# A hybrid attention block on one core: the order in which VectorE normalises the recurrence's output and TensorE turns it ahead of the first output projection

## The reference

```python
def mixer_ab(...):
    z = u @ w_in
    ...
    ya = diff_attention(qa, ka, va, lam, subln_g, lambda_init)   # 1024 columns
    yb = rwkv7_time_mix(zb, ...)                                 # 1024 columns
    return jnp.concatenate([ya, yb], axis=-1) @ w_out            # 2048 x 2048

# the end of rwkv7_time_mix: y is the recurrence's output, 16 heads of 64
    mu_y = jnp.mean(y, axis=-1, keepdims=True)
    var_y = jnp.mean(jnp.square(y - mu_y), axis=-1, keepdims=True)
    y = (y - mu_y) * lax.rsqrt(var_y + LNX_EPS)
    y = y * lnx_g + lnx_b
    y = (y + bonus) * g
```

## Time and profile before

| what | value |
|---|---|
| median of 3 runs | 2513.8 us (2513.76 to 2515.22) |
| the profiled execution's own time | 2517.1 us |
| its span in the trace | 2515.4 us |
| PE busy | 2477.1 us, 98% |
| DVE busy | 1502.9 us, 60% |
| ACT busy | 1202.0 us, 48% |
| POOL busy | 150.8 us, 6% |
| mean granted clock of PE | 0.996 of 2.4 GHz |
| stretch of the change | about 440 to 492 us from the span's start |

### The profile page before, as it was taken

The page is one execution under the profiler, slowest core; times in us unless marked ns, Lnnn a source line. Parts: engine busy times, 40 slices in busy tenths (PEclk is TensorE's granted clock), DMA queues, the critical chain, the costliest instruction groups (busy, mean ns, idle before and its releaser), DMA issues.

```text
span 2515.4 us, 32703 instructions
## 1 busy us (share of the span) xinstructions
PE 2477.1 (98%) x13517; PEld 2059.6 (82%) x13517; DVE 1502.9 (60%) x1986; ACT 1202.0 (48%) x1661; POOL 150.8 (6%) x173
## 2 busy tenths in 40 slices
PE   9999999999999999999999999999999999999998
PEld 7888778888888888888888977788888888888886
DVE  5556775766555555555566778556555555555565
ACT  6445432565345345354445556555435445445453
POOL 4001224100000000000100000000000000000000
PEclk9999999999999999999999999999999999999999
DMA  8556511655555555555554654455555565565554
GB/s 275 184 183 209 176 31 70 239 167 186 192 191 186 191 192 184 193 192 193 184 201 147 202 165 151 149 174 184 184 196 189 184 197 189 184 197 188 193 189 146
DMA packets 225145, 454.33 MB, mean 181 GB/s; under 512 B 7897, under 2 KB 16407, under 8 KB 223723
## 3 DMA queue, kind: packets, MB, share of 16 engines
q1 hardware_dynamic: 219165, 430.63, 52.3%
q0 software_dynamic: 3936, 18.59, 2.2%
q10 hardware_dynamic: 1902, 3.07, 0.4%
HBM read 446.57 MB, written 2.10 MB: 178 GB/s over the span
## 4 chain that ended last, share of the span: by engine, by line
PE 92%; DVE 5%; ACT 1%; issue 1%; DMA 0%; SPq 0%; DVEq 0%; ACTq 0%
PE psum L324 28%; PE psum L326 28%; PE psum L325 28%; DVE wlo L303 1%; PE psum L859 1%; PE psum L1882 1%; PE psum L1891 1%; PE psum L483 1%; ACT whi L292 0%; DVE h L678 0%; PE psum L1871 0%; DMA h<-in_x 0%; PE psum L1202 0%; PE psum L1203 0%; PE psum L1204 0%
## 5 line engine op out<-in xcount | busy, mean ns | idle before, releaser
L324 PE MATMUL psum<-whi,uTh 128*128 128x512 f32 (+2 forms) x2176 | 849.9, 391 | 6.3 <-DVE uTl L495 2.1
L326 PE MATMUL psum<-whi,uTl 128*128 128x512 f32 (+2 forms) x2176 | 841.8, 387 | 0.0
L325 PE MATMUL psum<-wlo,uTh 128*128 128x512 f32 (+2 forms) x2176 | 841.0, 386 | 0.0
L303 DVE TENSOR_TENSOR wlo<-raw,whi 128x2048 fp32r<-128x2048 f32 (+1 forms) x243 | 563.9, 2331 | 400.9 <-ACT whi L292 400.9
L292 ACT ACTIVATE whi<-raw 128x2048 fp32r<-128x2048 f32 (+1 forms) x243 | 462.9, 1913 | 414.2 <-DMA raw<-in_w_mlp_down 322.9
L307 DVE SCALAR_TENSOR_TENSOR wlo<-raw,gpre,whi 128x512 fp32r<-128x512 f32 (+1 forms) x656 | 441.7, 735 | 280.0 <-ACT whi L295 279.8
L295 ACT ACTIVATE whi<-raw,gpre 128x512 fp32r<-128x512 f32 (+1 forms) x656 | 414.3, 707 | 269.2 <-DMA raw<-in_w_mlp_up 245.4
L324 PEld LDWEIGHTS psum<-whi,uTh 128*128 128x128 f32 x2176 | 409.0, 188 | 92.9 <-issue 7.2
L326 PEld LDWEIGHTS psum<-whi,uTl 128*128 128x128 f32 x2176 | 408.8, 188 | 81.5
L325 PEld LDWEIGHTS psum<-wlo,uTh 128*128 128x128 f32 x2176 | 409.1, 188 | 78.4 <-issue 0.5
L324 PE MATMUL psum<-whi,hTh 128*128 128x512 f32 x1024 | 399.9, 390 | 0.0
(11 more groups left out here) (379 smaller groups left out, 1504.2 us busy)
## 6 DMA issues: line engine op xcount, KB each, us to landing
raw<-in_w_mlp_up SPq DMA_DIRECT2D x128, 1024.0 KB, 5.5
raw<-in_w_mlp_down SPq DMA_DIRECT2D x128, 1024.0 KB, 5.0
raw<-in_ab_w_in SPq DMA_DIRECT2D x48, 1024.0 KB, 5.2
raw<-in_w_ple_gate SPq DMA_DIRECT2D x32, 1024.0 KB, 5.1
raw<-in_c_w_in SPq DMA_DIRECT2D x24, 1024.0 KB, 5.3
raw<-in_ab_w_out SPq DMA_DIRECT2D x16, 1024.0 KB, 5.3
raw<-in_c_w_out SPq DMA_DIRECT2D x16, 1024.0 KB, 5.1
raw<-in_c_w_in SPq DMA_DIRECT2D x12, 736.0 KB, 4.6
```

Of the source, the lines that this page charges most:

```text
L303: dve.tensor_tensor(wlo[:, q, :, 0:n], raw[:, q, :, 0:n], whi[:, q, :, 0:n].bitcast(F32), ALU.subtract).then_inc(lo_ready, 1)
L324: pe.matmul(o, xh, hi, start=(q == 0 and k == 0), stop=False)
L325: pe.matmul(o, xh, lo, start=False, stop=False)
L326: last = pe.matmul(o, xl, hi, start=False, stop=(q == 3 and k == 3))
```

## The change

Four things are reordered; no instruction is added or removed, and every size stays.

1. DVE, before PE's first matmul of the stage: the rest of the second half of block 0 (`T_dve` 0, part 1) comes ahead of tile 0's Newton steps (k = 3) and no longer behind them.
2. DVE's norm goes by column and no longer by tile: the first column half (k = 4) of both tiles, and only after block 2's turn the second half (k = 5) of both.
3. PE's chunks of v = 1 go (0, 2), (1, 2), (0, 3), (1, 3), so block 3 is first needed by the third of them; block 3 is turned in the middle of v = 1's second chunk and no longer at the end of v = 0's fourth. Block 2 is turned where it was. `y_ready` counts `yb_done` by the new order, and `out_keep_act` of column block 0 waits for one chunk more.
4. ACT: `split_hi` of chunks 2 and 3 comes ahead of the squares of tile 1; `split_hi` of slab s+1's chunks 1 and 2 ahead of block 3's turn; `split_hi` of slab s+2's chunk 0 ahead of the eviction of column block 0.

```diff
-    OUT_CHUNKS = (((0, 0), (0, 1), (1, 0), (1, 1)), ((0, 2), (0, 3), (1, 2), (1, 3)))
+    OUT_CHUNKS = (((0, 0), (0, 1), (1, 0), (1, 1)), ((0, 2), (1, 2), (0, 3), (1, 3)))
@@ out_act
             T_act(act, st, 1)
-            y_square_act(act, 1)
             split_hi(act, s, 2)
             split_hi(act, s, 3)
+            y_square_act(act, 1)
             split_hi(act, s + 1, 0)
             T_act(act, st, 2)
-            T_act(act, st, 3)
             split_hi(act, s + 1, 1)
             split_hi(act, s + 1, 2)
+            T_act(act, st, 3)
             split_hi(act, s + 1, 3)
-            out_keep_act(act, st, 0, 4 * s + 6)
             split_hi(act, s + 2, 0)
+            out_keep_act(act, st, 0, 4 * s + 7)
             split_hi(act, s + 2, 1)
             out_keep_act(act, st, 1, 4 * s + 8)
@@ out_dve
-            out_norm_dve(dve, link, 0, 4)
             T_dve(dve, st, 1)
             out_norm_dve(dve, link, 1, 0)
             out_norm_dve(dve, link, 1, 1)
-            out_norm_dve(dve, link, 0, 5)
+            out_norm_dve(dve, link, 0, 4)
             split_lo(dve, s, 2)
             split_lo(dve, s, 3)
             out_norm_dve(dve, link, 1, 2)
             out_norm_dve(dve, link, 1, 3)
             out_norm_dve(dve, link, 1, 4)
+            split_lo(dve, s + 1, 0)
+            T_dve(dve, st, 2)
+            split_lo(dve, s + 1, 1)
+            out_norm_dve(dve, link, 0, 5)
             out_norm_dve(dve, link, 1, 5)
-            T_dve(dve, st, 2)
-            split_lo(dve, s + 1, 0)
+            split_lo(dve, s + 1, 2)
             T_dve(dve, st, 3)
-            for q in range(1, 4):
-                split_lo(dve, s + 1, q)
+            split_lo(dve, s + 1, 3)
             split_lo(dve, s + 2, 0)
             split_lo(dve, s + 2, 1)
@@ out_pair_pe
-                    if v == 0 and q == 3 and k % 2:
-
-                        if k == 3:
-                            last.then_inc(mm_used, 1)
-                        T_pe(pe, st, src, ready, 2 + k // 2)
-                if v or q < 3:
-                    last.then_inc(mm_used, 1)
+                    if k == 1 and (v, q) in ((0, 3), (1, 1)):
+                        T_pe(pe, st, src, ready, 2 + v)
+                last.then_inc(mm_used, 1)
@@ rwkv_dve
         out_norm_dve(dve, link, 0, 2)
+        T_dve(dve, "ab_out", 0, None, (1,))
         out_norm_dve(dve, link, 0, 3)
-        T_dve(dve, "ab_out", 0, None, (1,))
@@ y_ready
-            return lambda tt, b: (sem("ya_done"), tt + 1) if b < 2 else (sem("yb_done"), 2 * tt + b - 1)
+            return lambda tt, b: (sem("ya_done"), tt + 1) if b < 2 else (sem("yb_done"), 2 * (b - 2) + tt + 1)
```

## The result

The changed kernel takes 2516.97 us (median of 22 runs, 2515.13 to 2524.07), the kernel before 2513.73 us (22 runs, 2512.08 to 2517.04). The ratio is 1.0015, with a 95% interval of 1.0009 to 1.0021: slower, by 2 to 5 us, where 2.4 us less were forecast, and outside the range.

The account below looks back on a forecast made before the run. PE was taken to bound the kernel (92% of the span); PE waits removed, 1.19 + 0.35 + 0.84 = 2.38 us, brought the median from 2513.8 to a forecast 2511.4 us, range 2509.7 to 2514.3.

Parts of the forecast that it names:

- first term: Stage start: block 0's second half made earlier on DVE lets PE begin at 443.69 instead of 444.88, saving 1.19 us.
- The three terms: PE waits removed: 1.19 us at the stage's start, 0.35 us at chunk 3, 0.84 us around block 3's turn.
- The reading that DVE would find ACT's half ready: Block 0's second half: ACT has it at 441.46, before DVE ends the sums of squares at 441.53.
- The load: Slab s+2's chunk 1, issued at 478.6 into POOL's loads, takes 10.8 us, lands at 489.4 and costs nothing.
- its other end: Latest landing of slab s+2's chunk 1: 15.1 us after POOL began, at 493.0, a stall of 2.5 us.
- chunk 1 of slab s+2 lands late: Rival, chance 0.10: PE idles before slab s+2's second chunk; landing at 493.0 gives 2513.9 us, no gain or slower.
- within 0.2%: Whole kernel: chance 0.92 that the time is the same within 0.2% (5.0 us); faster 0.05, slower 0.03.
- The estimate from the page: POOL's loads and slab s+2's chunk: 2.0 us plus 4.46 MB over 436 GB/s from 477.9 ends at 490.1, just in time.
- First matmul 0.8 us behind the turn: Sign at the stage's start: PE's first matmul comes about 0.8 us behind the start of block 1's turn.
- No wait before chunk 3: Sign in the stage: chunk 3's rest is there at 453.1, wanted at 454.75, so the 0.23 us wait goes.
- Turns followed by matmuls at once: Sign: block 2's turn at about 462.9 and block 3's at 474.7 are each followed by matmuls at once.
- one sign of being wrong: Stated failure sign: the prediction is wrong if PE waits in slab s+2; no size given.

Follow-up runs that it names:

- before_gpost_held: Kernel before, with POOL's third load (gpost, 1024 KB) held until slab s+2's chunk 0 is used: 2514.72 us, ratio 1.0000.
- half_turn_alone: Kernel before with only the second half of block 0 moved ahead of tile 0's Newton steps on DVE: 2516.56 us, ratio 1.0006.
- before_pool_ahead: Kernel before with POOL's three loads held to start just ahead of slab s+2's chunk 0: 2516.41 us, ratio 1.0005.
- pool_on_norm: Changed kernel with POOL's three loads let go earlier, by the norm's last half instead of block 3's rest: 2512.59 us, ratio 0.9990.
- gpost_held: Changed kernel with POOL's third load (gpost, 1024 KB) held until slab s+2's chunk 0 is used: 2513.45 us, ratio 0.9990.
- pool_behind: Changed kernel with POOL's three loads held to start behind slab s+2's chunk 1 and ahead of chunk 2: 2514.42 us, ratio 0.9999.
- busy_wait: Changed kernel with 20 useless 128x128 matmuls on PE ahead of the wait for slab s+2's chunk 1: 2516.64 us, ratio 1.0006.
- changed_again: The changed kernel measured once more, without a further edit, beside the kernel before on another chip: 2516.59 us, ratio 1.0008.
- before_pool_late: Kernel before with POOL's three loads held until ACT's high part of slab s+1's last chunk: 2515.04 us, ratio 0.9997.
- norm_and_held_2: Second run: changed kernel with POOL's wple and pin loads let go by the norm's last half, gpost held until s+2's chunk 0 is used: 2512.11 us, ratio 0.9992.

## Why the prediction was wrong

**The stage itself: right in its mechanism, with a first term that one execution had made large.** The three terms, 1.19 + 0.35 + 0.84 = 2.38 us, measured 2.42 us in the changed kernel and 2.45 us where nothing comes after them, each against the one profile of the kernel before. The order of events came within 0.2 us once both are counted from block 1's turn: block 2's turn at 20.03 us (forecast 20.02), block 3's at 31.83 us (31.83), slab s+2 at 46.32 us (46.36). DVE was 0.9 us ahead at both turned blocks (0.8 forecast). But the close agreement is in part luck. The 1.19 us were read in an execution with a low clock in the recurrence; at the full clock the first matmul comes 1.19 us behind the turn even without part 1, so the term is 0.34 us, and the stage's gain 1.61 us (before_gpost_held). The reading that DVE would find ACT's half ready (441.46 against 441.53) had 0.07 us to spare, and the changed kernel's DVE waited 0.84 us for it. That the first term is one sum with the others, and worth nothing alone, was not said, and half_turn_alone shows it.

**The load: the step that failed.** The prediction put it: "With 10.8 us it lands at 489.4 and costs nothing: this value I take, since it is a like load in the same traffic." It was no like load. 10.8 us was the flight of a chunk issued when POOL's loads were 4.3 us under way. The chunk now came 0.8 us behind their first issue and had 3.5 us more of them ahead of it. What stays the same is not the flight but the landing behind POOL's first issue, 15.1 us, the number that the prediction had worked out as its other end and left. With it the landing is 477.9 + 15.1 = 493.0, forecast by its own clock, and 492.1 by the trace's, 0.8 us of which is the earlier recurrence. before_pool_ahead, pool_on_norm, gpost_held and pool_behind each move one side of this and PE's wait follows.

**The price of the wait: too low.** The rival "chunk 1 of slab s+2 lands late" named place and idle time (2.5 us, measured 2.37) but priced it at the idle alone, so that its end was "no change" (2513.9). The wait is also followed by 3 us at half the clock, which cost 1.66 us by the comparison with busy_wait. In the stretch the case costs 4.3 us instead of 2.5, and so lies above the kernel before by 1.9 us. This rival had a chance of 0.10 and should have been the main case.

**What stays open.** The medians of the first comparison lie 3.2 us apart (by the interval 2.3 to 5.3), those of changed_again 2.6 us, and the stretch is 1.9 us longer against the one profile of the kernel before, which is outside the first interval. Against its order at the full clock in the recurrence it is 2.7 us longer, which fits both. In how many of the timed runs of either kernel the clock was low there is not known, so this is the likely account and not a shown one. Some runs of the changed kernel, 2519 to 2524 us, have a mean granted clock of 0.993 to 0.995 where most have 0.996 to 0.997. They are not the late load's mark: the kernel before has such runs too (2519.1 to 2521.6 us, most at 0.994 or 0.995), and so has half_turn_alone (2524.2 and 2524.4 us, 0.993). That the chances were put on "within 0.2%" (0.92) agrees with the ratio of 1.0015, though for the wrong sum.

**The estimate from the page.** The Trainium skill, DMA: Bandwidth & Descriptors, section on the anatomy of one DMA, gave 12.2 us from POOL's first issue for all the bytes; the runs show 14.0 to 16.8 us. The section gives its rule for one transfer, and the prediction applied it to the sum of four in two queues. The measurement decides: in the changed kernel the estimate was 2.9 us short, more than the whole wait. Nor did the trace of before agree with it, as the prediction said: there the same bytes took 15.1 us, counted in the same way.

**Each sign named in advance.** First matmul 0.8 us behind the turn: 0.85. No wait before chunk 3: none. Turns followed by matmuls at once: yes. POOL's loads 35.0 us behind block 1's turn (477.9 - 442.9): 34.9. Chunk 1 with about 10.8 us in flight: 14.3, wrong. And one sign of being wrong that it named came: PE waited in slab s+2.

## What to carry to other kernels

When an engine finishes sooner, list the transfers that its signals let go, and place each beside the loads issued within the next microseconds: here 3328 KB that started just ahead of a tight load delayed it by 8 to 9.5 us, and the same bytes started just behind it did nothing to it. Take for a load in a crowd the landing counted from the crowd's first issue, not the flight of some other load in it, and leave it 2 us of play. Price a wait of the bound engine with what comes behind it too: 2.4 us of idle PE cost 4.3 us here, while 1.24 us cost 1.5. And look at the clock ahead of the stretch before taking a wait from one profile: a low clock there had made this one 0.8 us longer than it is in other executions.

## What the runs showed of the hardware

A 1 MB load of SP's queue issued 0.7 to 0.9 us behind three loads of POOL's queue (3328 KB) took 13.1 to 14.5 us in four traces; issued 0.7 and 2.7 us ahead of them it took 5.0 and 5.2 us. The queues did not share evenly; the order of issue decided.

PE's granted clock fell to its lower level (0.50) for some 3 us after an idle time of 2.37 and 2.39 us in slab s+2, when PE had already been at work again for over a microsecond; after idle times of 1.24 and 1.11 us there, or with useless matmuls in place of the idle time, it did not. The length of the idle time alone does not decide it: in the recurrence, at about 424 us, where PE's matmuls are of 64x64, it fell behind 1.50 us (the kernel before) and with 2.33 us (before_pool_late, before_pool_ahead, pool_behind), and stayed full with 2.33 us (pool_on_norm) and 2.48 us (norm_and_held_2).
